# Two-layer encoder trunk with gathered experts: VectorE's dot products read x from PSUM instead of SBUF

## The reference, cut to what matters

```python
def block_fn(args):                      # xb: 128 tokens, eb: their 8*16 experts, gb: their gates
    xb, eb, gb = args
    u = u_tab[eb]                        # 128 rows of 2048 f32 for each token
    h = jnp.einsum("thkd,td->thk", u, xb)
    coef = gb * jax.nn.gelu(h, approximate=False)
    return jnp.einsum("thk,thkd->td", coef, v_tab[eb])
```

## Time and profile before

| | |
|---|---|
| median of 3 timed runs | 3703.89 us (3697.67 to 3709.7) |
| the profiled execution's own time | 3707.39 us |
| its span, first to last instruction | 3705.7 us |
| instructions | 32338 |
| DVE busy | 2809.0 us, 76% |
| POOL busy | 2165.9 us, 58% |
| PE busy | 2132.5 us, 58% |
| ACT busy | 588.5 us, 16% |
| moved by DMA | 1106.71 MB, 299 GB/s over the span |

### The profile page before, as it was taken

One profiled execution on the slowest core, in us unless ns is written; L12 is line 12 of the kernel. 1 busy time (PEld: TensorE's weight loads), 2 busy tenths in 40 slices (PEclk: granted clock), 3 DMA queues, 4 the chain that ended last, 5 costly groups with the idle time before them and its releaser, 6 DMA issues. The chain is left out here.

```text
span 3705.7 us, 32338 instructions
## 1 busy us (share of the span) xinstructions
PE 2132.5 (58%) x8985; PEld 1496.3 (40%) x8985; DVE 2809.0 (76%) x3476; ACT 588.5 (16%) x1079; POOL 2165.9 (58%) x1470
## 2 busy tenths in 40 slices
PE   8968890000111489999499998900001113799993
PEld 7855790000111354444297976900001113544441
DVE  4997589898999766666733545898989998666667
ACT  1002430000111430000033543300001113400000
POOL 6794175888777447767400001758787774477774
PEclk9987995555555589999799999955555555799997
DMA  7421447999999569999755334479999995599997
GB/s 242 143 84 62 142 149 306 395 409 381 422 421 419 201 231 410 408 409 403 291 201 183 126 126 148 145 304 392 412 364 418 422 420 220 210 404 407 409 407 299
DMA packets 293725, 1106.71 MB, mean 299 GB/s; under 512 B 21957, under 2 KB 120837, under 8 KB 220677
## 3 DMA queue, kind: packets, MB, share of 16 engines
q0 software_dynamic: 147456, 805.37, 54.4%
q1 hardware_dynamic: 146182, 300.22, 22.5%
HBM read 1103.41 MB, written 2.10 MB: 298 GB/s over the span
## 5 line engine op out<-in xcount | busy, mean ns | idle before, releaser
L1270 DVE SCALAR_TENSOR_TENSOR ring<-ring,x_tok 128x2048 f32<-128x2048 f32 x512 | 1147.7, 2288 | 56.8 <-DMA ring<-in_peer_u,index_now 53.3
L510 POOL DMA_INDIRECT ring<-in_peer_u,index_now x512 | 961.1, 1877 | 329.6 <-DVE ring L1270 152.9
L733 PE MATMUL ps<-all_v,mix 128*128 128x512 f32 x1984 | 851.8, 592 | 0.0
L531 POOL DMA_INDIRECT work<-in_peer_v,index_add x344 | 455.2, 1323 | 321.4 <-DVE x_tok L1294 174.7
L1294 DVE SCALAR_TENSOR_TENSOR x_tok<-work,coef,x_tok 128x1024 f32<-128x1024 f32 x344 | 441.6, 1286 | 240.2 <-DMA work<-in_peer_v,index_add 238.9
L733 PEld LDWEIGHTS ps<-all_v,mix 128*128 128x128 f32 x1984 | 377.0, 190 | 474.5 <-issue 474.5
L717 PE MATMUL ps<-hot,hot 128*128 128x128 f32 x1024 | 229.9, 411 | 568.2 <-ACT hot L928 568.1
L477 POOL TENSOR_TENSOR w_lo<-ring,w_hi 128x2048 fp32r<-128x2048 f32 x34 | 159.1, 4683 | 663.9 <-ACT w_hi L831 663.9
L717 PEld LDWEIGHTS ps<-hot,hot 128*128 128x128 f32 x1024 | 209.8, 311 | 588.5 <-ACT hot L928 588.5
L707 PE MATMUL ps<-ident,coef 128*128 128x128 f32 x4 | 1.9, 474 | 695.2 <-DVE coef L1288 695.2
L1103 DVE TENSOR_TENSOR w_lo<-ring,w_hi 128x2048 fp32r<-128x2048 f32 x78 | 178.8, 2292 | 264.8 <-ACT w_hi L831 264.8
(11 more groups left out here) (171 smaller groups left out, 2878.0 us busy)
## 6 DMA issues: line engine op xcount, KB each, us to landing
all_v<-in_peer_v SPq DMA_DIRECT2D x248, 512.0 KB, 6.7
ring<-in_conv_w_in SPq DMA_DIRECT2D x16, 2048.0 KB, 8.6
ring<-in_peer_w_q SPq DMA_DIRECT2D x16, 2048.0 KB, 8.3
ring<-in_attn_w_kv SPq DMA_DIRECT2D x16, 2048.0 KB, 8.3
ring<-in_conv_w_out SPq DMA_DIRECT2D x8, 2048.0 KB, 7.7
ring<-in_attn_w_q SPq DMA_DIRECT2D x8, 2048.0 KB, 8.4
ring<-in_attn_w_o SPq DMA_DIRECT2D x8, 2048.0 KB, 7.8
ring<-in_peer_u,index_now POOLq DMA_INDIRECT x512, 9.9
```

The costliest lines, as they stand in the source:

```text
L510: pool.indirect_dma_start(u_tile(s), None, u_tab, bass.IndirectOffsetOnAxis(ap=index_now[:, half, s:s + 1], axis=0)).then_inc(u_row[s], 16)
L531: pool.indirect_dma_start(add_tile(k), None, v_tab, bass.IndirectOffsetOnAxis(ap=index_add[:, half, k % TB, k // TB:k // TB + 1], axis=0)) ...
L733: mm = pe.matmul(ps[:, dense_bank(tb, q), :], mix[tb][:, row, :], tile[:, q * 512 - HALF:(q + 1) * 512 - HALF], start=False, stop=True, sk ...
L1270: dve.scalar_tensor_tensor(out=u_tile(s), in0=u_tile(s), scalar=1.0, in1=x_tok[:, tb, :], op0=ALU.mult, op1=ALU.mult, accum_out=coef[:, tb ...
```

## The change

ScalarE copies x of both token blocks from `x_tok` into PSUM once per layer, after the last score has been taken out: block 0 to banks 0 to 3, block 1 to banks 4 to 7. The dots take x from there. DVE waits for block 0's copy ahead of the first dot and for block 1's ahead of that block's first dot. As bank 2 holds x of block 0 until its dots are done, PE's two transposes of `row_e` move behind the wait for `coef_done`, for both token blocks.

```diff
+        x_copied = sem("x_copied")
+        def x_dots(tb):
+
+            return ps[:, Q * tb:Q * tb + Q, :].rearrange("p a b -> p (a b)")
...
                     if n:
                         pe.wait_ge(slot_taken, n)
+                    pe.wait_ge(coef_done, n + 1)
                     for c in range(2):
                         pe.transpose(ps[:, 2, c * P:(c + 1) * P], row_e[:, tb, c, :], ident[:, :])
-                    pe.wait_ge(coef_done, n + 1)
                     pe.transpose(ps[:, 2, 2 * P:3 * P], coef[:, tb, :], ident[:, :]).then_inc(slot_ready, 1)
...
                     if c == 2 * EARLY_HEADS:
                         exp_of(layer, 0, 0)
+                act.wait_ge(score_taken, 8 + HC * (layer + 1))
+                for tb in range(TB):
+                    act.activation(x_dots(tb), x_tok[:, tb, :], ACT.Copy).then_inc(x_copied, 1)
...
-                    dve.scalar_tensor_tensor(out=u_tile(s), in0=u_tile(s), scalar=1.0, in1=x_tok[:, tb, :],
+                    dve.scalar_tensor_tensor(out=u_tile(s), in0=u_tile(s), scalar=1.0, in1=x_dots(tb),
                                              op0=ALU.mult, op1=ALU.mult, accum_out=coef[:, tb, slot]).then_inc(u_used, 1)
...
                     if h == PH - 1:
+                        dve.wait_ge(x_copied, layer * TB + 1)
                         opening_dots(0, RING)
...
                 route_part(layer, 1, 1)
+                dve.wait_ge(x_copied, layer * TB + 2)
                 dots(1, 0, 1)
```

## The result

| | before | after |
|---|---|---|
| median of the timed runs beside each other | 3706.8 us (3697.67 to 3714.44) | 3667.03 us (3663.89 to 3671.01) |
| the profiled execution's own time | 3707.39 us | 3665.31 us |
| its span | 3705.7 us | 3663.5 us |
| DVE busy | 2809.0 us | 2801.8 us |
| POOL busy | 2165.9 us | 1647.4 us |

The ratio is 0.9888 with an interval of 0.987 to 0.9906: 1.1% faster, 39.8 us between the medians and 42.1 us between the two profiled executions.

The account below looks back on a forecast made before the run. POOL, each instruction held until a dot ends, was taken to bound block 0's stretch. Gains of 40.2 us less 1.0 for transposes, 39.2, gave 3668.2 from the profiled execution, 3664.7 from the median: forecast 3665 us, range 3652 to 3675.

Parts of the forecast that it names:

- (a): POOL beside dots: with one SBUF input per dot, gathers fall from 1.91-2.19 to 0.94 us, index copies from 1.78 to 0.19.
- (b): Block 0's stretch: the DMA bounds it at 2.50 us per gather, gaining 17.9 and 22.3 us; block 1's stretch gains nothing.
- (c): The dot's own time on DVE: unchanged with x in PSUM; upper bound 11 to 44 ns a dot, 12 us in all.
- (d): ACT's two copies of x into PSUM: 1.91 us each, at most double, finished 6 to 10 us before the first dot.
- (e): The two transposes behind `coef_done`: hidden for block 0, 0.5 us exposed for block 1, 1.0 us in two layers.
- second rival: POOL stays held by something else of long dots, such as their result: 3705 us, chance 0.12; half free 3685, chance 0.05.
- first rival: A dot reading PSUM is 44 to 65 ns dearer over 266 dots: 12 to 17 us back, 3677 to 3682, chance 0.13.
- lower bound of nothing: The least a dot could gain from PSUM: nothing, since 2.28 us was taken as the fixed pace of both operand places.
- slower rival: Dots read long PSUM operands at a lower rate: 26.6 us per 0.1 us a dot, 3718 at 0.2 us, chance 0.05.
- the aside in the second rival on index copies alone: If only index copies came free, POOL needs 20.8 us per eight gathers: about half the gain, 3685 us, chance 0.05.
- 22.4 us an eight: POOL's time for eight gathers with their index copy while dots are paced by landings, 2.80 us each; the DMA needs 20.0.

Follow-up runs that it names:

- run 1: The changed kernel with the dots reading x from `x_tok` in SBUF again, all else kept: 3707.52 us beside 3707.58, ratio 0.9998.
- runs 2 and 3: The changed kernel with x read from PSUM in one block only: block 0 alone 3674.11 us (ratio 0.99), block 1 alone 3704.09 us (ratio 0.9996).
- run 4: The changed kernel with both dot inputs in SBUF, block 0's products written to PSUM, ScalarE's x copies left out: 3711.98 us, ratio 1.0008 to the kernel before.
- runs 9 and 10: The changed kernel plus a spare one-column VectorE copy behind every dot, of block 0 in the first, block 1 in the second: 3668.9 and 3685.14 us.
- Run 7: The kernel before, x still in SBUF, with one index copy of 16 row numbers replacing two of 8: 3683.45 us beside 3708.89, ratio 0.9935.

## Why the prediction was right

The forecast was 3665 us and the median is 3667.03. By its steps:

| step | forecast | measured |
|---|---|---|
| (a) a gather on POOL beside dots | 0.94 us | median 0.94, mean 0.96 |
| (a) an index copy | 0.19 us | median 0.20, mean 0.30 |
| (b) landings in block 0's stretch | 2.50 us | 2.496 and 2.501 |
| (b) block 0's stretch shorter | 17.9 and 22.3 us | 18.7 and 22.7 |
| (b) block 1's stretch | unchanged | 0.9 us shorter per layer |
| (b) DVE's waits for gathered rows before dots | some 15 us | 19.3 us |
| (c) the dot | unchanged | 3 ns shorter (median), 5 ns closer together |
| (d) ScalarE's two copies | near 3.8 us, hidden | 3.68 us, hidden |
| (e) the transposes | 1.0 us exposed | 0.7 us |

(a) and (b) hold, and run 1 shows that they carry the whole gain, runs 2 and 3 that it lies in block 0. The second rival, POOL held by the dot's result, is refuted by run 4 as well as by the gathers at 0.94 us. The changed kernel's own trace has a second witness for the two inputs. Only 30 of its 512 gathers take over 1.1 us, and 28 of them run beside the masks (L1310), which read two SBUF tiles: 1.12 to 1.21 us beside instructions of 0.69. What was won was kept: the stages from dot 255 to the next layer's first dot took 1181.0 us before and 1181.7 after, those behind the last dot 603.5 and 602.4.

(c) The first rival, a dearer dot, did not come. The lower bound of nothing was a little off too, since the dots come 2.208 us apart and not 2.213. The line of the dots and the line of ScalarE's copies after (min/median/max ns):

```profile
L1278 DVE SCALAR_TENSOR_TENSOR ring<-ring,ps x512: 2279/2282/2290, 572.3 to 3058.8; 128x2048 f32<-128x2048 f32 x171
...
L915 ACT ACTIVATE ps<-x_tok x4: 1862/1872/1882, 558.3 to 2395.2; 128x2048 f32<-128x2048 f32 x4
```

With x in SBUF the median was 2285 and the maximum 2381 ns. The fixed price that the Trainium skill ("VectorE: DVE Perf Modes", the TRN2 errata) gives a PSUM source does not appear in a 2048-element operand either: 2282 against 2285 ns. The rule of the Trainium skill ("SBUF — State Buffer", Who interferes with whom), that VectorE with one SBUF input does not contend with a GpSimd instruction that reads SBUF and with two inputs does, fits the gathers: 0.94 us in the changed kernel, 1.9 to 2.2 in runs 1 and 4. The inference of the Trainium skill in the same section that writing descriptors is not touched by two inputs, taken as a forecast of the whole gather's time, is not borne out: 1.94 us in run 4. The gather waits near its start (run 4), as it would if the reading of its row numbers were held, but what it does in that moment no run here shows.

(d) ScalarE's copies end at 561.94 and the first dot starts at 572.3, 10 us later.

(e) DVE's wait for `by_slot` ahead of block 1's masks is seen directly, where before there was none:

```profile
1239.39 0.49 ACT L923 ACTIVATE by_slot<-ps 128x384 f32<-128x384 f32 x1 [1.38 <-PE ps L712]
1239.91 2.50 DVE L1310 TENSOR_TENSOR hot<-iota_f,by_slot 128x512 f32<-128x512 f32 x4 [0.38 <-ACT by_slot L923]
```

The slower rival's price, 26.6 us for each 0.1 us a dot, was tried in runs 9 and 10: 7.7 us a layer for 0.06 us, in block 1 alone. For two layers that is 15.4 us, against 16 by the forecast's rate. The rate was right, and so is the place: block 0 pays nothing.

What was mis-sized is the aside in the second rival on index copies alone. It said that with all of them free and the gathers still held the time would be 3685, about half of the gain; with half of them gone it was 3683.45 already. By its own figures, 1.6 of the 2.4 us between 22.4 and 20.0, it should have said two thirds, some 27 us, near 3680. The 22.4 us an eight is itself too much for the whole stretch: it is POOL's pace while dots are paced by landings, and over block 0's stretch before the change the landings came at 2.65 and 2.69 us in the two layers, 21.2 and 21.5 an eight. Run 7 shows 2.52 to 2.53 us per landing with 2.0 us gathers and half of the copies, against 2.50 with POOL free. So held gathers nearly keep up with the DMA, and the copies were what made POOL fall behind; that held gathers without any copy would keep up in full was not run. The forecast itself did not use the 22.4: it set the measured ends of the stretches against a pace of 2.50 us.

Between the two profiled executions the account is this. Block 0's stretches give 18.7 + 22.7 us, block 1's 1.8, and the routings between them 0.2. The first dot starts 1.6 us later (570.6 and 572.3; it lies at 570.1 to 573.3 in the other runs), and all stages behind dot 255 win 0.3, the 0.7 us lost to (e) included. That is the 42.1 us that was measured.

The mechanism is shown, but that the number came out within 2 us is in part luck. The forecast counts from where the stretches ended in one execution of the kernel before, 633.4 us for both layers together. With POOL held that sum was 625.4 in run 1 and 635.4 in run 4, so another execution of a kernel held in the same way could have moved the forecast by up to 8 us.

## What to carry to other kernels

A gather whose instruction takes twice as long beside one VectorE line as alone is probably held by that line; compare its minimum with its median, its period with the other line's, and its end with the end of the other line's instruction (here always 0.8 us apart). Before moving the operand, find the stretch in which the held engine is the bound (neither VectorE nor the transfers full there) and sum the gain from that stretch alone, up to the next limit. And once transfers bound a stretch, look for work that can be moved behind the start of its first transfer, to where the ring is in flight.

## What the runs showed of the hardware that was not expected

- A dot with its second input in PSUM comes every 2.208 us in close order in block 1, with both in SBUF every 2.213; the steps from dot to dot that hold the masks are 4.47 instead of 4.50 us. Together they make block 1's stretch 314.4 instead of 315.3 us in all runs that differ in this (run 10, with its spare copies, aside).
- Where POOL is late, the DMA engines are busy nearly all the time and still move less; which part of a transfer takes longer there, no run separated. Before the change the window from 680 to 720 us had the DMA engines busy for 0.95 of the time at 376 GB/s; after it the same window, with POOL ahead, 1.01 at 422. The two rows, before and after:

```profile
680.00:720.00 40.00, 0.00 (x0) 0.00 (x0) 31.91 (x29) 0.00 (x0) 34.09 (x18) 0.50 0.95 376
```
```profile
680.00:720.00 40.00, 0.00 (x0) 0.00 (x0) 37.14 (x33) 0.00 (x0) 15.78 (x19) 0.50 1.01 422
```

- With the result of the dots in PSUM and both inputs in SBUF (run 4), a dot of block 0 took 2315 ns in the mean, 22 more than before; whether it is the write or the wait for the dot before the last was not separated.
